# Letting the V half of an expert layer run 44 slots behind its U half, not 140, in a one-core trunk kernel

## The reference, cut to what matters

```
u      = rmsnorm(h) ; q = u @ w_query
top 16 of 128 keys on either side, top 16 of their 256 sums     (8 heads a token)
best_i = 16 x 8 = 128 experts a token, of 16384 ; gates = softmax(best scores)
ue, ve = expert_u[best_i], expert_v[best_i]                     (rows of 1024 floats)
act    = gelu(u . ue) * gates
h     += sum over the 128 experts of act * ve
h     += sigmoid(rmsnorm(h) @ w_gate) * (p @ w_proj)
```

## Time and profile before

| | |
|---|---|
| median of 3 runs | 3802.0 us |
| the profiled execution's own time | 3792.98 us |
| its span, first to last instruction | 3791.2 us |
| mean granted TensorE clock | 0.781 |
| busy share of PE, DVE, ACT, POOL | 65%, 59%, 17%, 52% |
| moved by DMA | 1320.00 MB, mean 348 GB/s |
| of it the gathers (queue q0) | 1073.87 MB |

### The profile page before, as it was taken

The page is one execution under the profiler, slowest core; times in us unless marked ns, Lnnn a source line. Parts: engine busy times, 40 slices in busy tenths (PEclk is TensorE's granted clock), DMA queues, the critical chain, the costliest instruction groups (busy, mean ns, idle before and its releaser), DMA issues. The chain is left out here.

```text
span 3791.2 us, 32350 instructions
## 1 busy us (share of the span) xinstructions
PE 2479.1 (65%) x10344; PEld 1197.6 (32%) x10344; DVE 2228.4 (59%) x5398; ACT 659.3 (17%) x1471; POOL 1953.7 (52%) x2064
## 2 busy tenths in 40 slices
PE   8869676769876687668777676777244534434565
PEld 5644345433434344223334343222011101101111
DVE  2341899774466766755567668655566666665200
ACT  3341222231212212201122113111000000100000
POOL 0000444444455565555566565656666666666563
PEclk9879887679987778788888777788556657756787
DMA  7315888879999999999999999999999999999996
GB/s 226 116 71 197 313 325 304 292 270 400 405 403 366 372 391 389 357 406 405 399 404 387 354 394 379 376 407 386 409 384 390 370 388 381 388 380 383 346 374 244
DMA packets 427455, 1320.00 MB, mean 348 GB/s; under 512 B 54280, under 2 KB 75920, under 8 KB 425112
## 3 DMA queue, kind: packets, MB, share of 16 engines
q0 software_dynamic: 294912, 1073.87, 73.6%
q1 hardware_dynamic: 132376, 244.06, 17.7%
HBM read 1290.69 MB, written 32.60 MB: 349 GB/s over the span
## 5 line engine op out<-in xcount | busy, mean ns | idle before, releaser
L1577 DVE CUSTOM_DVE_ANT_0 u_ring<-u_ring,ps 128x1024 f32<-128x1024 f32 x1024 | 1229.7, 1217 | 510.1 <-DMA u_ring<-peer_u,idx_u 434.3
L870 POOL DMA_INDIRECT u_ring<-peer_u,idx_u x1024 | 977.4, 954 | 1036.9 <-DVE dots L1577 409.3
L886 POOL DMA_INDIRECT v_ring<-peer_v,idx_v x984 | 933.3, 948 | 739.5 <-PE ps L2009 289.1
L2009 PE MATMUL ps<-v_ring,spread 128*32 128x512 f32 x3936 | 733.7, 877 | 870.8 <-DMA v_ring<-peer_v,idx_v 788.4
L2009 PEld LDWEIGHTS ps<-v_ring,spread 128*32 128x32 f32 x3936 | 146.1, 139 | 1277.5 <-issue 1265.6
L1755 PE MATMUL ps<-front 128*128 128x512 f32 x1024 | 457.1, 603 | 2.0 <-ACT front L1123 2.0
L1755 PEld LDWEIGHTS ps<-front 128*128 128x128 f32 x1024 | 194.7, 194 | 268.7 <-issue 268.6
L1951 PE MATMUL ps<-front 128*128 128x512 f32 x512 | 232.0, 611 | 13.2 <-DVE front L1493 13.2
L1874 PE MATMUL ps<-front 128*128 128x256 f32 x768 | 196.4, 413 | 9.2 <-DVE a_max L1359 7.7
L1874 PEld LDWEIGHTS ps<-front 128*128 128x128 f32 x768 | 155.8, 209 | 62.4 <-issue 39.2
L1951 PEld LDWEIGHTS ps<-front 128*128 128x128 f32 x512 | 98.9, 197 | 150.6 <-issue 150.6
(11 more groups left out here) (235 smaller groups left out, 2661.1 us busy)
## 6 DMA issues: line engine op xcount, KB each, us to landing
front<-w_in SPq DMA_DIRECT2D x76, 1024.0 KB
front<-w_out SPq DMA_DIRECT2D x32, 1024.0 KB
front<-peer_w_query SPq DMA_DIRECT2D x32, 1024.0 KB
u_ring<-peer_u,idx_u POOLq DMA_INDIRECT x1024
v_ring<-peer_v,idx_v POOLq DMA_INDIRECT x984
front<-c_bias_all SPq DMA_DIRECT2D x32, 320.0 KB
front<-x SPq DMA_DIRECT2D x16, 512.0 KB
front<-cs_rows SPq DMA_DIRECT2D x8, 1024.0 KB
```

The lines of the kernel that those rows point to most:

```text
L870: nc.gpsimd.indirect_dma_start(k.u_ring[:, n % RU, :], None, io["peer_u"][0], bass.IndirectOffsetOnAxis(ap=k.idx_u[:, t % 2, j:j + 1], axi ...
L886: nc.gpsimd.indirect_dma_start(row, None, io["peer_v"][0], bass.IndirectOffsetOnAxis(ap=k.idx_v[:, t % 2, token:token + 1], axis=0)).then_ ...
L1577: nc.vector.tensor_tensor_reduce(out=row, in0=row, in1=k.un_ps, scale=1.0, scalar=0.0, op0=ALU.mult, op1=ALU.add, accum_out=k.dots[:, t % ...
L2009: last = mm(k.acc_ps[32 * j:32 * j + 32, half * 512:(half + 1) * 512], centres[:, at:at + 32], row[:, half * 512:(half + 1) * 512], start= ...
```

## The change

Two heads of a tile are 32 experts a token. The change fetches V per two heads: a V row now holds 32 experts of each of four tokens (partition = token of four x 32 + expert). Eight such rows carry the two heads of 32 tokens, 32 rows those of 128 tokens. V can start once 32 dots are there, so V row n is fetched in slot n + 44 (`BEHIND` = 32 + 12). The steps of the chain are done per part of 32 dots in place of 128. The sparse matrix gets four weight columns per row in place of one; the number and the shape of the matmuls in `values` stay. The last V rows keep the ring of 8.

```diff
-TAIL, RT = SEQ - P, RV + 4
+PART = 2 * TOPK
+PARTS = KK // PART
+BEHIND = PART + LAG
-SLOTS = SEQ + P + LAG
+SLOTS = SEQ + BEHIND
...
-    if t < TILES and h == PH - 1 and s == TOPK - 1:
-        out += [("gelu", t)] + ([("un", t + 1)] if t < LAST else [])
-    if 1 <= t <= TILES and h == 0 and s == 1:
-        out.append(("weigh", t - 1))
-    if t >= 2 and h == 0:
-        if s == 2:
-            out.append(("res_in", t - 2))
-        if s == LAG:
-            out.append(("add", t - 2))
+    if n < SEQ and n % PART == PART - 1:
+        out.append(("gelu", n // PART))
+    if t < LAST and h == PH - 1 and s == TOPK - 1:
+        out.append(("un", t + 1))
+    if PART < n <= SEQ + 1 and n % PART == 1:
+        out.append(("weigh", n // PART - 1))
+    done = n - P - BEHIND
+    if done % P == P - 10 and done > -P:
+        out.append(("res_in", done // P + 1))
+    if done % P == 0 and done >= 0:
+        out.append(("add", done // P))
+    row = n + 3 - BEHIND
+    if 0 <= row < SEQ and row % (EDGE * Q) == 0:
+        out.append(("spread", row // (EDGE * Q)))
...
-GATE_AT = [752, 804, 856, 908, 960, 1012, 1060]
+GATE_AT = [722, 768, 814, 860, 906, 952, 998]
 def slot_time(n):
-    full = P + LAG
+    full = BEHIND
     return 1.3 * min(n, full) + 2.6 * max(0, n - full)
...
-        pool = range(4) if n >= 100 else range(6) if vacated else range(8)
+        pool = range(4) if n >= 25 else range(6) if vacated else range(8)
...
 def gather_v(n):
-        if n >= TAIL + RT:
-            pool.wait_ge(k.v_free, (n - RT) // Q + 1)
-        elif n >= TAIL + RV:
-            pool.wait_ge(k.u_free, SEQ)
-        elif n >= RV:
+        if n >= RV:
             pool.wait_ge(k.v_free, (n - RV) // Q + 1)
...
-        act_fn(k.dots[:, t % 2, :], k.dots[:, t % 2, :], ACT.Gelu).then_inc(k.gelu_full, 1)
+        part = k.dots[:, m // PARTS % 2, m % PARTS * PART:(m % PARTS + 1) * PART]
+        act_fn(part, part, ACT.Gelu).then_inc(k.gelu_full, 1)
...
-        act_fn(spread[:, e % 2, :, :, 0], k.wT[:].rearrange("k (q c) -> k c q", q=Q)[:, e * EDGE:(e + 1) * EDGE, :],
-               ACT.Copy).then_inc(k.spread_full, 1)
+        for s in range(Q):
+            own = slice(s * PART, (s + 1) * PART)
+            src = k.wT[own, :].rearrange("k (q c) -> k c q", q=Q)[:, b % 2 * EDGE:(b % 2 + 1) * EDGE, :]
+            act_fn(spread[own, b % 2, :, :, s], src, ACT.Copy).then_inc(k.spread_full, 1)
...
+    def turn_part(ps, src):
+        for s in range(Q):
+            last = mm(ps[s * PART:(s + 1) * PART, 0:PART], src, every_fourth[:, s, :], start=True, stop=True)
+        return last
```

More of the change, by code:

```diff
@@ L262, in beside_slots @@
     put(FRONT_SPANS[-1][1], ("g_load",))
-    for t in range(TILES):
-        put(t * P + 99, ("rows", t))
-        put(t * P + P + 6, ("w_turn", t))
+    for m in range(TILES * PARTS):
+        put(m * PART + 25, ("rows", m))
+        put(m * PART + PART + 6, ("w_turn", m))
     for t, n in enumerate(GATE_AT):
@@ L602, in v_slot @@
     def v_slot(self, n):
[L604 to L609, removed]
+        return self.v_ring[:, n % RV, :], self.v_in[n % RV], n // RV * 16 + 16
 def sync_program(nc, sp, k, io):
@@ L873, in gather_v @@
     def gather_v(n):
[L874 to L877, removed]
+        m, r = divmod(n, PART)
+        column = r % Q * (PART // Q) + r // Q
+        if r == 0:
+            b = k.bank["rows", m]
             pool.wait_ge(k.copied[b.place], b.done)
-        if n >= TAIL + RT:
-            pool.wait_ge(k.v_free, (n - RT) // Q + 1)
-        elif n >= TAIL + RV:
-            pool.wait_ge(k.u_free, SEQ)
-        elif n >= RV:
+        if n >= RV:
             pool.wait_ge(k.v_free, (n - RV) // Q + 1)
@@ L1549, in top @@
             if kk >= 2 * PH:
-                b = k.bank["rows", kk // PH - 2]
+                b = k.bank["rows", (kk - 2 * PH) // 2]
                 dve.wait_ge(k.filled[b.place], b.n + 1)
@@ L1562, in g_norm, with rows_of_values @@
         ts(k.gates[:, kk // PH % 2, at:at + TOPK], k.gexp[:], k.gsum[:, 0:1], None, ALU.mult).then_inc(k.gates_full, 1)
-    def rows_of_values(t):
-        _, ps, copied_ = filled(("rows", t))
-        if t >= 2:
-            n = (t - 1) * P - 1
-            dve.wait_ge(k.v_in[n % RV], n // RV * 16 + 16)
-        nc.vector.tensor_copy(k.idx_v[:, t % 2, :], ps[:, 0:P]).then_inc(copied_, 1)
+    def rows_of_values(m):
+        _, ps, copied_ = filled(("rows", m))
+        if m >= 2:
+            _, here, count = k.v_slot((m - 1) * PART - 1)
+            dve.wait_ge(here, count)
+        nc.vector.tensor_copy(k.idx_v[:, m % 2, :], ps[:, 0:PART]).then_inc(copied_, 1)
     def dot(n):
@@ L1578, in dot, with weigh @@
                                        accum_out=k.dots[:, t % 2, j:j + 1]).then_inc(k.u_free, 1)
-    def weigh(t):
-        dve.wait_ge(k.gelu_full, t + 1)
-        dve.wait_ge(k.gates_full, (t + 1) * PH)
-        if t:
-            b = k.bank["w_turn", t - 1]
+    def weigh(m):
+        dve.wait_ge(k.gelu_full, m + 1)
+        dve.wait_ge(k.gates_full, 2 * (m + 1))
+        if m >= PARTS:
+            b = k.bank["w_turn", m - PARTS]
             dve.wait_ge(k.filled[b.place], b.n + 1)
-        tt(k.weights[:], k.dots[:, t % 2, :], k.gates[:, t % 2, :], ALU.mult).then_inc(k.weights_full, 1)
+        t, part = m // PARTS, slice(m % PARTS * PART, (m % PARTS + 1) * PART)
+        tt(k.weights[:, part], k.dots[:, t % 2, part], k.gates[:, t % 2, part], ALU.mult).then_inc(k.weights_full, 1)
     def add_values(t):
@@ L1978, in q_s, with rows_of_values, w_turn @@
         last.then_inc(filled, 1)
[L1982 to L1990 removed]
+    every_fourth = ident.rearrange("p (x s) -> p s x", s=Q)
+    def turn_part(ps, src):
+        for s in range(Q):
+            last = mm(ps[s * PART:(s + 1) * PART, 0:PART], src, every_fourth[:, s, :], start=True, stop=True)
+        return last
+    def rows_of_values(m):
+        pe.wait_ge(k.idx_full, 2 * (m + 1))
+        ps, filled = open_(("rows", m))
+        turn_part(ps, k.row_f[:, m // PARTS % 2, m % PARTS * PART:(m % PARTS + 1) * PART]).then_inc(filled, 1)
+    def w_turn(m):
+        pe.wait_ge(k.weights_full, m + 1)
+        ps, filled = open_(("w_turn", m))
+        turn_part(ps, k.weights[:, m % PARTS * PART:(m % PARTS + 1) * PART]).then_inc(filled, 1)
     def values(t, c):
         if c % EDGE == 0:
[L1995 removed]
+            pe.wait_ge(k.spread_full, Q * ((t * STEPS + c) // EDGE + 1))
         if c == 0:
```

54 lines of the change are left out of this document (20 added, 34 removed).

## The result

The changed kernel takes 3756.5 us (median of 4 runs, 3753.05 to 3758.27) against 3798.7 us for the kernel before (4 runs, 3789.34 to 3802.16): ratio 0.9892, 95% interval 0.9871 to 0.9912. It is faster, by 42 us. The forecast was 3715 us with a range of 3675 to 3772. So the direction and the range held, and the size was off by a factor of two: 78 us of gain were forecast.

A forecast was written before the change was run, and what follows sets the result against it. The prediction took DMA at 386 to 388 GB/s as the bound with U and V together, DVE with U alone. Terms +53 (slots 22 to 204), +11 (204 to 1023) and -142 (tail) gave -78: 3715 us, range 3675 to 3772.

The forecast's parts named there:

- The cycle of the small ring: Tail: 44 V rows in a ring of 8 take 6.5 us a group, 82 us in all, so -142 us.
- the handovers: Slots 204 to 1023: added gelu, spread and other chain steps hide in idle time, taken at 0, between -10 and +30.
- slots 204 to 1023: Stages after the front of group 1: gates moved in from the tail add 4.4 MB at 388 GB/s, +11 us.
- I take 600 us: Slots 22 to 204: 224.9 MB with V beside the front take 600 us, +53, bounds 580 to 660.
- straight line between the densities: Slots 22 to 204: rate interpolated between 388 and 341 GB/s by front density, giving 367 GB/s and 613 us.
- DMA is the bound: Stages with U and V together: DMA share 1.00 at 386 to 388 GB/s means DMA limits them.
- so there is room: Slots 22 to 204: POOL needs 2 x 1.24 us per slot and a slot takes 3.3 us.
- A: Rival: group 1 stays tangled at 293 GB/s, its stretch takes 768 us, whole time 3883 us; chance 0.07.
- B: Rival: half tangled, slots 22 to 204 run at 341 GB/s and take 660 us, whole time 3775; chance 0.13.
- C: Rival: the small ring costs the tail its dear bound, 115 us at 9.5 us a group, whole time 3748; chance 0.08.
- D: Rival: 24 added rounds of handovers cost 2 us each, 48 us, whole time 3763; chance 0.07.
- E: Rival: no bytes are saved, so nothing moves, gain below 0.5%; chance 0.05.

The follow-up runs named there:

- before_ring8: The kernel before with the ring of 8 rows throughout the tail of 140 V rows: 3862.34 us, ratio 1.0131.
- after_ring12: The changed kernel with the tail's ring of 12 rows given back: 3753.41 us, ratio 0.9854 against the kernel before.
- parts_140: The changed kernel with V put back to 140 slots behind U; gates, PSUM banks and residual waits as in the kernel before: 3867.3 us, ratio 1.0134.
- after_gelu_copy: The changed kernel with a plain copy in place of the gelu of the 32 parts: 3658.81 us, ratio 0.9862 against the kernel before.
- after_pace: The changed kernel with 1.5 times the planned cost for the chunked attention's and scan's steps, so they stand thinner: 3654.86 us, ratio 0.9860.
- the two versions for group 1: The changed kernel with the ring of 12 and 1.5 or 2.0 times those steps' planned cost in group 1 only: 3746.38 and 3740.02 us.
- half_v_rows: The changed kernel with half of each V row gathered, all instructions otherwise as many and as long: ratio 0.9518 against the kernel before.
- skip3_v_rows: The changed kernel with three of four V gathers left out, the matmuls kept: 3060.45 us, ratio 0.8249 against the kernel before.

## Why the prediction was right or wrong, point by point

**Right: the place of the gain.** V rows came out of a tail in which they stood alone and went beside U; the tail lost 136.9 us where -142 was forecast. The cycle of the small ring was worked out as 6.1 to 7.0 us a group and is 7.0; I took 6.5.

**Right: the handovers and slots 204 to 1023.** +11 forecast, +5 by the second profile of before, +7 between `before_ring8` and `after_ring12` of one chip, +20 by the first pair. `parts_140` measures the handovers at 5 to 8 us, `after_gelu_copy` the table loads at nothing.

**Wrong: the step "I take 600 us" for slots 22 to 204.** They took 621.5 (620.9 on another chip), +73 to +74 and not +53. This is the largest term of the miss: between the two profiles the gain is 40 us in place of 78, and of the 38 missing 21 are here, 9 in slots 204 to 1023, 5 in the tail, 3 at both ends. The prediction's own straight line between the densities gave 367 GB/s and 613 us, and the windows show 366 GB/s; it was set aside because slots 172 to 204 ran at 394. Those slots are the weight-heavy ones, with a DMA share of 1.01 and more in every run that has all its gathers; they say nothing of the chunked attention's and the scan's steps, which fell within slots 96 to 172. These 76 slots took 280.8 us at 340 GB/s. At the 388 GB/s of the forecast their bytes would take 246: the 35 us between are about all that the whole stretch lies above its bytes at 388 GB/s (227.5 MB, 586 us). The dose of their density (642 us crowded, 621 as it is) shows that these steps cost more when they stand closer. That thinner is better (607) showed in `after_pace` only, and hardly in the two versions for group 1.

**Wrong underneath: "DMA is the bound".** The rate of 386 to 388 GB/s was read from stages with a DMA share of 1.00 and taken for a full DMA. A full DMA is 405 to 409 GB/s, as in slots 172 to 204 of the changed kernel. The quiet slots of a chip with pauses, as the forecast's base was (187.5 us of them), did not feel over a fifth fewer bytes in `half_v_rows`: POOL's issue with its pauses held them. On a chip without pauses DMA is the bound as the prediction said, at 406 GB/s. For slots 204 to 1023 this mattered little, as the gathers per slot stayed two.

For slots 22 to 204 the prediction set POOL's need, 2 x 1.24 us a slot, against the mean slot ("so there is room"). It left out that after each stop of the front POOL has to refill the rings at that pace. Whether this is what the missing term was is argued and not shown: POOL waited 201 of the 621.5 us for rows, so it had room in the mean. How the 73 us divide, by differences of single profiles, partly from different chips: 27 by half of V's bytes; 19 by half of its gathers, up to 12 of them pauses; 5 by a further quarter of its gathers with their bytes; 21 stay with fewer gathers than the kernel before had. For these 21 stand V's matmuls (all there in `skip3_v_rows`, PE busy 450.6 us against 397.1), the handovers, the four banks and the front's new places. No run separates them, and the cause stays open.

**Signs of being wrong.** Of the signs set out, the rate (366 GB/s), DVE's load (66%), slots 204 to 1023 (2582.3 us at 384 GB/s) and the tail (86.9 us) came as named. The first V gather (478.3), the start of slot 204 (1051.7) and the page's GB/s (315 to 355 in slices eight to ten, where 370 and more was named) did not.

**The base.** The sum was made against an execution of 3793 us; the same kernel's median was 3798.7 beside the changed one, and its second profiled execution took 3810.7. By the second profile the kernels are 58 us apart, by the first 40, by the medians 42.

**The rivals.** A (293 GB/s throughout) is out, with 366. B (341 GB/s, 660 us) stood nearest: its rate held for slots 96 to 172 (340), not for all. C, 9.5 us a group, is out, with 7.0. D, 2 us a handover, is out, with 5 to 8 us for all. E, no gain, is out, with 42 us.

The Trainium skill ("SBUF — State Buffer", section "SBUF: two separate sides") has the rule that a DMA issued from GpSimd can't write its descriptors while VectorE runs a two-port operation. The median V gather stayed at 941 ns, the longest took 1994, so no run here bears it out as a cost of the change. The Trainium skill ("DMA: Bandwidth & Descriptors", section "Bandwidth") gives 358 GB/s for a core's share of HBM and 425 as measured on a core that streams alone. The 405 to 409 GB/s of this case's one core lie above the first and below the second.

## What to carry to other kernels

A DMA share of 0.98 to 1.00 didn't prove that bytes were the bound: divide the stage by the number of issues first, and if the issuing engine shows no waits but its own, it is the bound. Here the two were so close (707 us of issuing, 799 of a stage at full DMA) that the chip decided. When a stream is moved beside other work, price the dense part of that work by its own rate, not by the neighbour that happens to be bound by something else. A ring that holds two of the groups in which its rows are freed can run at the pace of its own cycle (release, issue, landing, use): here 7.0 us a group, and 5.1 with a third group.

## What the runs showed of the hardware that was not expected

On some chips POOL pauses about 3 us, in slots 708 to 1000 once in 14 to 18 gathers, with nothing of the program to wait for. POOL's timeline of the changed kernel (start, us, instruction, idle before):

```profile
3014.16 0.94 POOL L868 DMA_INDIRECT u_ring<-peer_u,idx_u  x1 [0.30 <-issue]
3018.06 0.94 POOL L880 DMA_INDIRECT v_ring<-peer_v,idx_v  x1 [2.96 <-remote]
...
3037.65 0.94 POOL L868 DMA_INDIRECT u_ring<-peer_u,idx_u  x1 [0.30 <-issue]
3040.90 0.94 POOL L880 DMA_INDIRECT v_ring<-peer_v,idx_v  x1 [2.32 <-remote]
```

Before V gathers they sum to 173.4 us in this run and to 187.5 in the kernel before; in slots 22 to 204 of this run there is a single one, of 2.0 us. The four kernels on the chip on which the kernel before took 3709 us show none at all, and their slots 708 to 1000 take 798 to 802 us at 406 to 407 GB/s in place of 856. What the pauses are, and why some chips have none, the profile doesn't tell.
